# The last modulation group of a two-block transformer kernel: the sum over row pairs moved from TensorE to ScalarE and VectorE

## The reference, cut to what matters

```python
mod = jax.nn.silu(c) @ w_ada[l] + b_ada[l]          # (1,1024) @ (1024, 6144)
sh1, sc1, ga1, sh2, sc2, ga2 = jnp.split(mod, 6, axis=-1)
h = modulate(rms_norm(x, g_norm1[l]), sh1, sc1)     # x*(1+scale)+shift
...                                                  # attention, short convolution, gates
x = x + ga1[:, None, :] * (merged @ w_o[l])
h2 = modulate(rms_norm(x, g_norm2[l]), sh2, sc2)
x = x + ga2[:, None, :] * hierarchical_moe(h2, ...)
```

## Time and profile before

| | |
|---|---|
| median of 3 runs | 1148.68 us |
| the profiled execution, its own time | 1147.94 us |
| its span in the profile | 1146.1 us |
| TensorE busy | 97% |
| VectorE busy | 42% |
| ScalarE busy | 36% |
| GpSimd busy | 16% |
| DMA | 331.75 MB, mean 289 GB/s |
| chain of waits | PE 89%, DMA 4%, DVE 3%, ACT 2%, SP's queue 2% |

### The profile page before, as it was taken

How to read it: one execution, slowest core, us unless ns; L and a number is a source line. 1 busy time by engine, 2 the same in 40 slices (tenths; PEclk the granted TensorE clock), 3 DMA queues, 4 the chain that set the end, 5 groups by cost and what they waited for, 6 DMA issues and landing times.

```text
span 1146.1 us, 15442 instructions
## 1 busy us (share of the span) xinstructions
PE 1116.1 (97%) x5860; PEld 752.1 (66%) x5860; DVE 483.6 (42%) x966; ACT 414.6 (36%) x616; POOL 184.3 (16%) x79
## 2 busy tenths in 40 slices
PE   5899999999999999999999998999999999999998
PEld 3689777874444444444444445978878888888876
DVE  4686344662222222222222214789574653233136
ACT  4543553331111111111111115675464454444234
POOL 0303233000000000000000002100314064342522
PEclk9999999999999999999999999999999999999999
DMA  9968668789999999999999996452434366455451
GB/s 354 381 223 296 215 245 313 285 347 418 421 424 423 422 422 424 423 424 423 423 422 423 424 423 254 148 200 99 143 121 160 124 207 207 150 180 211 158 183 37
DMA packets 96830, 331.75 MB, mean 289 GB/s; under 512 B 8529, under 2 KB 31298, under 8 KB 71170
## 3 DMA queue, kind: packets, MB, share of 16 engines
q1 hardware_dynamic: 96496, 330.58, 74.4%
q0 software_dynamic: 80, 0.26, 0.1%
q10 hardware_dynamic: 194, 0.06, 0.0%
HBM read 329.84 MB, written 1.05 MB: 289 GB/s over the span
## 4 chain that ended last, share of the span: by engine, by line
PE 89%; DMA 4%; DVE 3%; ACT 2%; SPq 2%; issue 1%; DVEq 0%; ACTq 0%
PE ps L1273 19%; PE ps L904 15%; PE ps L905 14%; PE ps L906 14%; PE ps L1313 9%; DMA ring<-in_w_in 4%; PE ps L1250 3%; PE ps L1251 2%; PE ps L1328 1%; PE ps L979 1%; SPq L773 1%; PE ps L1329 1%; DVE ring_r L2110 1%; PE ps L1436 1%; ACT ring_r L1648 1%
## 5 line engine op out<-in xcount | busy, mean ns | idle before, releaser
L866 POOL TENSOR_TENSOR ring_r<-ring,ring_r 128x1024 fp32r<-128x1024 f32 x66 | 172.0, 2627 | 840.4 <-ACT ring_r L1648 840.3
L905 PE MATMUL ps<-ring_r,hl_r 128*128 128x512 f32 x528 | 209.1, 396 | 0.0
L904 PE MATMUL ps<-ring_r,hl_r 128*128 128x512 f32 x480 | 195.2, 407 | 5.6 <-DVE hr_r L2202 4.3
L906 PE MATMUL ps<-ring_r,hr_r 128*128 128x512 f32 x480 | 190.2, 396 | 0.0
L1648 ACT ACTIVATE ring_r<-ring 128x2048 fp32r<-128x2048 f32 x88 | 163.6, 1908 | 59.0 <-PE ps L906 44.7
L2110 DVE TENSOR_TENSOR ring_r<-ring,ring_r 128x2048 fp32r<-128x2048 f32 x55 | 129.6, 2367 | 81.6 <-ACT ring_r L1648 81.3
L1273 PE MATMUL ps<-ring,arena 128*64 128x512 f32 x688 | 153.3, 594 | 0.7 <-DMA ring<-in_w 0.7
L905 PEld LDWEIGHTS ps<-ring_r,hl_r 128*128 128x128 f32 x528 | 99.6, 189 | 21.6
L904 PEld LDWEIGHTS ps<-ring_r,hl_r 128*128 128x128 f32 x480 | 90.5, 188 | 32.1 <-issue 6.3
L1273 PEld LDWEIGHTS ps<-ring,arena 128*64 128x64 f32 x688 | 48.4, 137 | 92.7 <-issue 89.7
L906 PEld LDWEIGHTS ps<-ring_r,hr_r 128*128 128x128 f32 x480 | 90.4, 188 | 21.9
(11 more groups left out here) (381 smaller groups left out, 1820.1 us busy)
## 6 DMA issues: line engine op xcount, KB each, us to landing
ring<-in_w SPq DMA_DIRECT2D x64, 2048.0 KB, 23.1
ring<-in_w_in SPq DMA_DIRECT2D x20, 2048.0 KB, 10.8
gates<-in_w SPq DMA_DIRECT2D x22, 1024.0 KB, 22.8
ring<-in_w_ada SPq DMA_DIRECT2D x16, 1024.0 KB, 9.5
arena<-in_w SPq DMA_DIRECT2D x11, 1024.0 KB, 19.7
uy<-in_w SPq DMA_DIRECT2D x11, 1024.0 KB, 21.7
ring<-in_w_ffn_gate SPq DMA_DIRECT2D x11, 1024.0 KB, 5.4
ring<-in_w_ffn_up SPq DMA_DIRECT2D x11, 1024.0 KB, 7.9
```

The source lines that it names most:

```text
L866: nc.gpsimd.tensor_tensor(rest[:, a:b], w[:, a:b], lead[:, a:b].bitcast(F32), ALU.subtract).then_inc(sem("w_rest_b"), 1)
L904: mm(o, lhsT=a_lead, rhs=b_lead, start=start, stop=False, skip_group_check=True)
L905: mm(o, lhsT=a_lead, rhs=b_rest, start=False, stop=False, skip_group_check=True)
L906: return mm(o, lhsT=a_rest, rhs=b_lead, start=False, stop=stop, skip_group_check=True)
```

## The change

The sum over a pair's two row blocks and their scaling by silu(c) leave TensorE, for group `g3` alone; group `g2` stays as it was.

ScalarE multiplies the pair's first row block by silu(c) in place, one scalar for each partition (`pair_scaled`, one instruction of 128x2048), behind the attention work of `gate00`, `gate10`, `gate20`, `gate30`. VectorE multiplies the second row block by its silu(c) and adds the first (`pair_summed`, one instruction of 128x2048) at the end of its steps 5, 7 and 9 and, for the last pair, ahead of the rest part of `pa`. TensorE then waits for that and sums over the 128 partitions with a constant of ones: four matmuls of 512 columns instead of eight. All 32 rows of a PSUM strip now hold the sum; the code behind reads the one it read before.

```diff
@@ TensorE
             def late_pair(group, n):
                 o = small.claim(pe, f"{group}_{n}")
-                modulation_pair(group, n, o, True, True).then_inc(small.done, 1)
+                if group == "g2":
+                    modulation_pair(group, n, o, True, True).then_inc(small.done, 1)
+                    return
+                pe.wait_ge(sem("pair_summed"), n + 1)
+                w = pair_of(slot_of[f"{group}_{n}"])
+                for i in range(4):
+                    last = mm(o[32 * i:32 * i + 32, :], lhsT=ones[:, 0:32], rhs=w[:, 0, i * COL:(i + 1) * COL], start=True,
+                              stop=True)
+                last.then_inc(small.done, 1)
@@ ScalarE
+            def pair_scaled(n):
+
+                w = pair_of(arrived(act_, f"g3_{n}"))[:, 0, :]
+                act_.wait_ge(sem("cpad_ready"), 1)
+                af(w, w, ACT.Identity, scale=sc_c[:, 3, 2 * n:2 * n + 1]).then_inc(sem("pair_scaled"), 1)
...
                 if unit in PAIR_AT and PAIR_AT[unit][1] == 0:
                     modulation_sums(PAIR_AT[unit][0])
+                if unit[:4] == "gate" and u == 0:
+                    pair_scaled(int(unit[4]))
                 if unit == "gate00":
@@ VectorE
+            def pair_summed(n):
+
+                w = pair_of(slot_of[f"g3_{n}"])
+                dve.wait_ge(sem("pair_scaled"), n + 1)
+                v.scalar_tensor_tensor(w[:, 0, :], w[:, 1, :], sc_c[:, 3, 2 * n + 1:2 * n + 2], w[:, 0, :], ALU.mult,
+                                       ALU.add).then_inc(sem("pair_summed"), 1)
...
+                if n in (5, 7, 9):
+                    pair_summed(n // 2 - 2)
                 if n in (0, 2, 4, 6, 8):
                     rest_weights(M["bg"] + n // 2)
 
+            pair_summed(3)
             rest_weights(M["pa"])
             modulation_sums("g3", 3)
             rest_weights(M["pb"])
@@ two semaphores fewer: scale1_ready and scale2_ready become scales_ready, hf_exp and hf_ln become hf_steps, as in
-            pe.wait_ge(sem("scale2_ready"), 1)
+            pe.wait_ge(sem("scales_ready"), 3)
```

More of the change, by code:

```diff
@@ L1715, in h1_leads @@
             def h1_leads(t, k0, n):
-                act_.wait_ge(sem("scale1_ready"), k0 // 4 + 1)
+                act_.wait_ge(sem("scales_ready"), k0 // 4 + 1)
                 for k in range(k0, k0 + n):
@@ L1882, in _ @@
                     act_.wait_ge(sem("hf_scaled"), u + 1)
-                    af(two_tiles(khT, u), two_tiles(khT, u), ACT.Exp, scale=-1.0).then_inc(sem("hf_exp"), 1)
+                    af(two_tiles(khT, u), two_tiles(khT, u), ACT.Exp, scale=-1.0).then_inc(sem("hf_steps"), 1)
                     if u == 1:
-                        act_.wait_ge(sem("hf_exp"), 2)
-                        af(khT, khT, ACT.Ln, bias=1.0).then_inc(sem("hf_ln"), 1)
+                        act_.wait_ge(sem("hf_steps"), 2)
+                        af(khT, khT, ACT.Ln, bias=1.0).then_inc(sem("hf_steps"), 1)
                         act_.wait_ge(sem("fox_exp_ln"), 1)
@@ L1889, in _ @@
                         lead_weights(M["fk"], (0,))
-                        act_.wait_ge(sem("hf_ln"), 1)
+                        act_.wait_ge(sem("hf_steps"), 3)
                         af(QE[0], khT, ACT.Exp, scale=-1.0).then_inc(sem("sigmoid_ready"), 1)
@@ L2188, in first_scales @@
                 v.scalar_tensor_tensor(scale1[:, 4 * h:4 * h + 4], mod[:, KD + 4 * h:KD + 4 * h + 4], 1.0, pc("g_norm1", 4 * h, 4),
-                                       ALU.add, ALU.mult).then_inc(sem("scale1_ready"), 1)
-                dve.wait_ge(sem("scale1_ready"), h + 1)
+                                       ALU.add, ALU.mult).then_inc(sem("scales_ready"), 1)
+                dve.wait_ge(sem("scales_ready"), h + 1)
                 dve.wait_ge(sem("xnT_ready"), 2 * h + 2)
@@ L2311, in _ @@
             v.scalar_tensor_tensor(scale2[:, :], mod[:, 4 * KD:5 * KD], 1.0, ffnmod[:, 2, :], ALU.add,
-                                   ALU.mult).then_inc(sem("scale2_ready"), 1)
-            dve.wait_ge(sem("scale2_ready"), 1)
+                                   ALU.mult).then_inc(sem("scales_ready"), 1)
+            dve.wait_ge(sem("scales_ready"), 3)
             dve.wait_ge(sem("route_in"), 96)
```

## The result

The changed kernel took 1158.75 us (median of 4 runs, 1156.18 to 1163.58), the kernel before beside it 1148.35 (4 runs): a ratio of 1.0092, 95% interval 1.0079 to 1.0106. Run again later, 1157.44 against 1148.79 us, ratio 1.0066 (1.0046 to 1.0086). The forecast was +2.8 us; the measured loss is 10.4 us the first time and 8.7 the second. The profiled execution took 1163.58 us, its span is 1161.8 us, so it is one of the longer ones; the profile of the second time took 1160.96. Lines have moved: the new matmuls are L991, ScalarE's scaling L1737, VectorE's sum L2238, its rest parts L2126; L1279, L1281 and L1273 of before are L1287, L1289 and L1281.

What follows compares the result with a forecast made beforehand. TensorE's queue, busy 97% of the span, was taken as the bound. Shifts of 0.43 + 2.81 - 0.76 + 0.5 = 3.0 us, taken as 2.8, on 1148.68 gave 1151.5 us, range 1149.0 to 1153.8.

Steps and rivals of the forecast that it cites:

- What the change gives and adds: At the `g3` pairs: four matmuls take 0.97 us instead of 1.85, 3.5 saved in all; ScalarE adds 2.00, VectorE 2.35.
- Pairs 0 to 3 and `pa`: TensorE's waits for the sums: 1.3 us, 3.7, none, none, then 1.3 at `pa`, whose first product is late by 3.0.
- The clock, rival one: TensorE's clock falls to half in the new 3.7 us gap at pair 1, losing 1.65 us: 1153.2; chance 0.10.
- The shift passes one to one: From `pa` through the experts' stage to the end, TensorE's lateness of 3.0 us arrives in full.
- the rival "faster": At all four pairs the sums are ready when TensorE asks, gaining 3.5 us: 1145.2; chance 0.05.

Runs made afterwards that it cites:

- changed_start16: The changed kernel, its sums where they were, with 16 tiny overwritten matmuls in TensorE's idle time at the start; 1154.3 us, ratio 1.0044 to the kernel before.
- changed_pad16: The changed kernel with four tiny overwritten matmuls in front of each pair's four, behind the wait for the sum; 1153.5 us, ratio 1.0049 to the kernel before.
- before_again: The kernel before run once more, unaltered; 1148.57 us, ratio 1.0001.

## Why the prediction was wrong

*What the change gives and adds.* Right. Four matmuls for 1.06 (1.00 to the next row) instead of 0.97, ScalarE 2.01 for 2.00, VectorE 2.35 for 2.35.

*Pairs 0 to 3 and `pa`.* Right in place and size: 1.20, 3.59, 0, 0.17 and 1.14 us of waiting, against 1.3, 3.7, 0, 0 and 1.3. With the clock kept up and the stream's length restored, the kernel takes 1151.8 us, or 1151.1 without the tiny matmuls in it. The forecast of 1151.5 is the time of that kernel, not of the one that was built.

*The clock, rival one.* Mis-sized in its chance. I gave it 0.10, with a price of 1.65 us. The price was about right (1.5 to 1.8 us, once 2.9), but it happened in all five profiles in which TensorE idles through the wait. I had set a gap of 6.14 us, which halved the clock, against one of 2.46, which I read as harmless; the new one of 3.6 lies between, and I let the lower neighbour decide without a reason, although the same trace has a wait of 2.34 us with the clock at 0.55 behind it, at 702. The rule of the Trainium skill ("TensorE: Matmul & The Clock Gate", section "What's actually happening"), told in the forecast, pointed the right way, and the falls behind the waits of 3.59 us agree with it. With the rival's 1153.2 as the forecast this step would have been right, and the time still too short by 4 to 6 us. Two kernels with this fall and a short gap behind the loop took 1153.5 (1152.1 without its tiny matmuls) and 1154.3.

*"The shift passes one to one".* This is the step that failed. I argued with the transfers, and they did pass it on (the lateness is the same at 251 and 560). But I took TensorE's own speed and stream behind `pa` as given. Two things broke that. The gap where TensorE leaves the experts' loop went from 1.7 to 7.3 us, through the 16 matmuls that the change removes: with tiny, overwritten ones in their place it is back at 1.44 to 2.00, and the kernel before with 16 fewer has it at 7.37 and nothing left of the 2.8 us by which it was ahead. The tiny ones are worth 3.4 us without the waits (1149.55 to 1146.14) and 3.1 with them (1157.44 to 1154.3). And the clock fell once more at 242 to 254, for 3.3 us in both profiles of the changed kernel, in a stretch that the forecast takes to run as before.

*Why the rival "faster" didn't come.* Its time, 1145.2, is nearly reached by the versions with early sums and a restored stream (1145.7 and 1146.1). Against the kernel before on their chips these gain 3.2 and 2.7 us of the 3.5; the place of the sums and the place of the code hid it.

*The sum.* By medians, with changed_start16 as the kernel with a short gap: 1148.8 for before, 2.3 us for the waits less the gains (1151.1), 3.2 for the two falls of the clock (1154.3), 3.1 for the gap behind the loop (1157.4). Of the 3.2, the lateness puts 1.5 to 1.8 at pair 1. The fall in the routing stage is 3.3 us where a profile has it and nothing where it hasn't, so what is left, some 1.5 us, would be its mean over executions; that is reckoned, not shown. Nor is the split between clock and gap firm. With changed_pad16 instead (1153.5, or 1152.1 without its tiny matmuls) the same sum gives 1.0 for the falls of the clock and 5.3 for the gap. The medians of the changed kernel and of these two are of four runs each, and those of one kernel lie 2 to 5 us apart.

What stays open: what decides whether the clock falls in the routing stage, and how much of the spread between runs it makes. That the long fall of 3.4 us shows in three of six profiles with the waits (the changed kernel's two and changed_start16) and in none without is a count, not a cause.

## What to carry to other kernels

Removing instructions moves all the code behind them. Where a long program leaves a loop for code that isn't loaded, here with the DMA queues full, look at the "issue" gap there before and after any edit, and try a few empty instructions at a place where the engine is idle anyway. It cost 0.3% here, about as much as the edit could give at best, and 4 tiny matmuls mended it.

A wait of 3.6 us on TensorE cost 1.5 us or more beyond its length. If it can't be avoided, fill it with matmuls into a bank that is overwritten; here that kept the clock up in the one profile taken.

Work that is handed to another engine is only free at the right place in that engine's queue: the same instructions took 8.2 us less with three of the four sums at other places (1154.3 against 1146.1).

## What the runs showed of the hardware that I had not expected

- TensorE goes on 2.4 to 2.6 us after the start of a 16 KB instruction load, and the next load comes 5.7 to 5.9 us after the first while the transfers run at a share of 1.0. Where TensorE has to wait for the second, the gap is 7.3 us instead of 1.6.
- The gap is a matter of a few instructions: 16 matmuls fewer give 7.3 us, 12 fewer 1.66, 24 fewer 1.71 and a later 0.56.
- PEclk can fall to 0.50 while TensorE is busy without a pause, at 244 to 254 in the changed kernel, among matmuls of 36 and 128 columns, and in other kernels not at all at the same work.
- A line with matmuls right behind a wait can still run at full pace (8 records in 1.06 us at 156.34 in changed_start16) while the clock falls just after them, at 157.4: the same wait, and a loss of 1.8 us that shows at another row.
- A wait of 2.3 to 2.8 us is followed by half the clock in some profiles and not in others: 2.46 us at 38 in before was not, 2.62 at the same place in before_again was.
